# A decay row by DMA in place of four turns, and a reordered front of each DeltaNet head

## The reference

```python
gc = jnp.cumsum(g, axis=-1)                       # log decay within a chunk of 64
diff = gc[..., :, None] - gc[..., None, :]
decay_incl = jnp.exp(jnp.where(incl, diff, -jnp.inf))
m = jnp.einsum('bhnid,bhnjd->bhnij', kb, k) * decay_strict
sol = lax.linalg.triangular_solve(eye + m, rhs, left_side=True, lower=True)
attn = jnp.einsum('bhnid,bhnjd->bhnij', q, k) * decay_incl
qd = q * jnp.exp(gc)[..., None]
...
o = rmsnorm(o, head_norm) * jax.nn.silu(g_out...)
```

## Time and profile before

| | us |
|---|---|
| median of 3 runs | 2720.67 (2720.61 to 2720.92) |
| profiled execution | 2720.52 |
| its span | 2718.7 |
| TensorE busy | 2705.3 |
| VectorE busy | 1581.7 |
| ScalarE busy | 1100.1 |
| GpSimd busy | 258.2 |

### The profile page before, as it was taken

The page is one execution under the profiler, slowest core; times in us unless marked ns, Lnnn a source line. Parts: engine busy times, 40 slices in busy tenths (PEclk is TensorE's granted clock), DMA queues, the critical chain, the costliest instruction groups (busy, mean ns, idle before and its releaser), DMA issues.

```text
span 2718.7 us, 35832 instructions
## 1 busy us (share of the span) xinstructions
PE 2705.3 (100%) x13096; PEld 2251.9 (83%) x13096; DVE 1581.7 (58%) x2504; ACT 1100.1 (40%) x1849; POOL 258.2 (9%) x231
## 2 busy tenths in 40 slices
PE   9999999999999999999999999999999999999998
PEld 7888878888887888888888888788888878888887
DVE  6554357888885345553355543688888943455532
ACT  4222247766663232222222222566676622322222
POOL 0000022122120010000000000211212100100000
PEclk9999999999999999999999999999999999999999
DMA  4223335554542222233322233455556332222332
GB/s 166 96 97 104 92 101 140 130 142 111 136 126 93 98 88 100 93 101 93 102 93 93 100 93 96 108 131 140 125 124 145 96 108 93 93 100 93 97 94 66
DMA packets 84603, 292.04 MB, mean 107 GB/s; under 512 B 10001, under 2 KB 12689, under 8 KB 84497
## 3 DMA queue, kind: packets, MB, share of 16 engines
q1 hardware_dynamic: 69232, 235.85, 26.5%
q0 software_dynamic: 14976, 54.53, 10.9%
q10 hardware_dynamic: 288, 0.27, 0.0%
HBM read 233.99 MB, written 2.10 MB: 87 GB/s over the span
## 4 chain that ended last, share of the span: by engine, by line
PE 97%; DVE 2%; ACT 0%; issue 0%; DMA 0%; DVEq 0%; POOLq 0%; POOL 0%; ACTq 0%
PE bank L438 95%; PE bank L637 1%; PE bank L689 1%; DVE c_lo L1747 0%; DVE w_lo L1235 0%; ACT c_hi L1191 0%; PE bank L651 0%; PE bank L725 0%; DVE sqb L1743 0%; DVE hf L1743 0%; DMA pcol<-in_params_in 0%; DVE hf L1738 0%; PE bank L458 0%; DVE NT L1664 0%; ACT w_hi L855 0%
## 5 line engine op out<-in xcount | busy, mean ns | idle before, releaser
L1235 DVE TENSOR_TENSOR w_lo<-raw,w_hi 128x1024 fp32r<-128x1024 f32 x342 | 422.6, 1237 | 542.2 <-ACT w_hi L855 542.1
L855 ACT ACTIVATE w_hi<-raw 128x1024 fp32r<-128x1024 f32 x446 | 469.8, 1055 | 658.7 <-PE bank L438 658.6
L438 PE MATMUL bank<-h_hi,w_hi 128*128 128x512 f32 x1504 | 587.1, 390 | 2.2 <-DVE h_lo L1260 2.1
L438 PE MATMUL bank<-h_hi,w_lo 128*128 128x512 f32 x1504 | 585.5, 389 | 0.0
L438 PE MATMUL bank<-h_lo,w_hi 128*128 128x512 f32 x1504 | 585.3, 389 | 0.0
L438 PE MATMUL bank<-g_hi,w_hi 128*128 128x512 f32 x928 | 384.2, 414 | 0.0
L438 PE MATMUL bank<-g_hi,w_lo 128*128 128x512 f32 x928 | 378.7, 408 | 0.0
L438 PE MATMUL bank<-g_lo,w_hi 128*128 128x512 f32 x928 | 369.6, 398 | 0.0
L438 PEld LDWEIGHTS bank<-h_hi,w_hi 128*128 128x128 f32 x1504 | 282.3, 188 | 63.3 <-issue 3.6
L438 PEld LDWEIGHTS bank<-h_hi,w_lo 128*128 128x128 f32 x1504 | 282.3, 188 | 58.8
L1535 DVE SCALAR_TENSOR_TENSOR cacc<-c_raw,ncol,cacc 128x512 f32<-128x512 f32 x464 | 330.0, 744 | 0.4
(11 more groups left out here) (258 smaller groups left out, 3355.5 us busy)
## 6 DMA issues: line engine op xcount, KB each, us to landing
raw<-in_w_in SPq DMA_DIRECT2D x128, 512.0 KB, 3.3
w_lo<-raw POOLq DMA_DIRECT2D x104, 512.0 KB, 4.6
raw<-in_ffn_w_gate SPq DMA_DIRECT2D x88, 512.0 KB, 3.2
raw<-in_ffn_w_up SPq DMA_DIRECT2D x88, 512.0 KB, 3.2
raw<-in_ffn_w_down SPq DMA_DIRECT2D x64, 512.0 KB, 3.5
raw<-in_ffn_w_down SPq DMA_DIRECT2D x32, 384.0 KB, 3.1
raw<-in_w_a_out SPq DMA_DIRECT2D x16, 512.0 KB, 3.2
raw<-in_w_b_out SPq DMA_DIRECT2D x16, 512.0 KB, 3.2
```

Source lines behind the costliest of these rows:

```text
L438: return nc.tensor.matmul(o, a, b, start=start, stop=stop, **kw)
L855: nc.scalar.activation(w_hi[c % SLOTS][:, :], raw[c % SLOTS][:, :], ACT.Copy).then_inc(hi_done, 1)
L1235: tt(w_lo[c % SLOTS][:, :], raw[c % SLOTS][:, :], w_hi[c % SLOTS][:, :].bitcast(F32), ALU.subtract).then_inc(lo_v, 1)
```

## The change

In the 14 later heads the four turns `gr` no longer run. At the first head of each layer a copy of gc of all heads is turned once on TensorE into 32 rows (bank 5), copied by ScalarE and written by a DMA to a scratch in HBM (`gc_rows`). For each later head a DMA issued by GpSimd reads its row back, the same row to all 128 partitions, into `dec`, after y3 of the head before. The exponential eg reads this row, and stands ahead of osq at the end of the head before. dmin reads `dec` instead of bank 0.

In the first head of a layer, eg comes ahead of ksq. On TensorE `so` moves behind `x2t`, and vt comes after one more `H`; two more `H` stand in front of x2t. On VectorE og and vE move behind vT. On GpSimd the sum of squares waits for dmin, and qd for vT.

```diff
-PE_ORDER = "H H gr kt H kk kq H so H H H x2t vt H H H xt0 y0 H H fb xy0".split()
+PE_ORDER = "H H gr kt H kk kq H H H H H H x2t so H vt xt0 y0 H H fb xy0".split()
...
-ACT_STEPS = ["thk", "thq", "XTI", "thv", "ksq", "eg", "decT", "kd", "n0", "n1"]
+ACT_STEPS = ["thk", "thq", "XTI", "thv", "eg", "ksq", "decT", "kd", "n0", "n1"]
...
+        gc_rows = nc.dram_tensor("gc_rows", (DEPTH, HEADS * NC, P), F32, kind="Internal").ap()
...
-                        m.then_inc(*pe_dn.step(name))
+                        m.then_inc(gr_done, 1)
+                        nc.tensor.transpose(bank[5][0:HEADS * NC, 0:P], abw[:, 4, :, :].rearrange("p h c -> p (h c)"), ident).then_inc(gct_pe, 1)
...
+                    if name == "gr" and rn != l * 8:
+                        return
...
+                    if rn == l * 8:
+                        act.wait_ge(gr_done, l + 1)
+                        nc.scalar.activation(qd[:, :], bank[0][:, :], ACT.Exp).then_inc(*ac_dn.step("eg"))
                     pe_("kt")
...
-                    nc.scalar.activation(qd[:, :], bank[0][:, :], ACT.Exp).then_inc(*ac_dn.step("eg"))
...
+                    if rn == l * 8:
+                        act.wait_ge(gct_pe, l + 1)
+                        nc.scalar.activation(S[0:HEADS * NC, :], bank[5][0:HEADS * NC, 0:P], ACT.Copy).then_inc(gct_a, 1)
...
                     pe_("os3")
+                    if not gates:
+                        act.wait_ge(row_in, (rn + 1 - l) * 16)
+                        nc.scalar.activation(qd[:, :], dec[:, :], ACT.Exp).then_inc(*ac_dn.step("eg"))
...
+                nc.vector.tensor_copy(abw[:, 4, :, :], sums[:, 0])
...
-                        pe_("gr")
+                        ac("eg")
+                        me("hs")
                         for c in range(NC):
-                            a = stt(out=dec[:, c * P:c * P + P], in0=bank[0][:, c * P:c * P + P], scalar=hs[:, HS_GC, c:c + 1], in1=cst[:, I_CAP, :],
+                            a = stt(out=dec[:, c * P:c * P + P], in0=(bank[0] if rn == l * 8 else dec)[:, c * P:c * P + P], scalar=hs[:, HS_GC, c:c + 1], in1=cst[:, I_CAP, :],
...
-                        if before:
-                            tail("og", rn - 1)
                         ac("ksq")
...
+                        act_of("v", va, va, thv)
                         if before:
+                            tail("og", rn - 1)
                             tail("vE", rn - 1)
-                        act_of("v", va, va, thv)
...
+                                    if rn == l * 8:
+                                        dve.wait_ge(gct_out, (l + 1) * 16)
...
-                            pool.wait_ge(pe_dn.sem, pe_dn.after(rn, "gr"))
+                            ve("dmin")
                             square_sum(rn - 1)
                         ac("eg")
-                        ve("neg")
+                        ve("vT" if before else "neg")
...
+                        if t == 0 and rn is not None and rn != l * 8 + 7:
+                            if rn == l * 8:
+                                pool.wait_ge(gct_a, l + 1)
+                                pool.dma_start(out=gc_rows[l], in_=S[0:HEADS * NC, :]).then_inc(gct_out, 16)
+                                pool.wait_ge(gct_out, (l + 1) * 16)
+                            pool.wait_ge(pe_dn.sem, pe_dn.after(rn, "y3"))
+                            h = rn + 1 - l * 8
+                            row = gc_rows[l, h * NC:h * NC + NC, :].rearrange("(o c) i -> o (c i)", o=1)
+                            pool.dma_start(out=dec[:, :], in_=row.broadcast_to([P, SEQ])).then_inc(row_in, 16)
```

More of the change, by code:

```diff
@@ L96 @@
 assert PE_ORDER.count("H") == 6 * HALVES, PE_ORDER.count("H")
-PE_STEPS = [x for x in PE_ORDER if x not in ("H", "so", "fb")]
+PE_STEPS = [x for x in PE_ORDER if x not in ("H", "gr", "so", "fb")]
 PE_TAIL = ["so", "fb"]
@@ L246, in trunk @@
         ghi_done = sem("ghi_done")
+        gr_done = sem("gr_done")
+        gct_pe = sem("gct_pe")
+        gct_a = sem("gct_a")
+        gct_out = sem("gct_out")
+        row_in = sem("row_in")
         mrinv_done = sem("mrinv_done")
```

## The result

| | before | after |
|---|---|---|
| median, us | 2720.86 (6 runs) | 2731.9 (6 runs) |
| profiled span, us | 2718.7 | 2729.4 |
| TensorE busy, us | 2705.3 | 2706.0 |
| TensorE idle ahead of xy0, as printed | none | 10.5 in 14 heads |

The change made the kernel slower by 11.0 us, a ratio of 1.0041 with a 95% interval of 1.0028 to 1.0053. The predicted 2722.5 and its range of 2717 to 2729 were too low; slower had been given 0.18.

A forecast was written before the change was run, and what follows sets the result against it. TensorE, busy 2705.3 of 2718.7 us, was taken as the bound. Twelve later heads +2.5, last heads 0, first heads -1.3, just in time +0.4, qd's touch 0.2: +1.8, so 2722.5 us, range 2717 to 2729.

The forecast's parts named there:

- There is a catch: VectorE beside GpSimd's sum: bnk2, with two SBUF inputs, ends 0.05 to 0.1 us behind the sum.
- The turns and the order: TensorE, later heads: without gr and with so directly behind x2t, a head would be 0.45 us shorter.
- x2t's wait: TensorE, later heads: x2t has 0.1 us to spare; a just-in-time start adds 0.4 us over 14 heads.
- xy0's wait: TensorE: xy0 waits 0.61 us for VectorE's yd0, 0.66 us a head with the longer matmul behind the wait.
- the wait as 0.21 shorter: Last head of each layer: no dcol, so the wait at xy0 is 0.21 us shorter, 0.45.
- 0.91 us of waiting a head: Upper case of the wait at xy0, with vE's start 0.25 us later: total +4.5 us.
- Rival B: GpSimd's sum, taking 1.8 us, becomes what x2t waits for, x2T 0.5 late: +7.4 us, 2728.1; chance 0.16.
- Rival A: No wait at xy0, VectorE's four taps covered: -7.6 us, 2713.1; chance 0.10, including a wait under 0.14 us.
- C: The power behind vE takes the port ahead of the first tap: taps 1.2 us later, 17 us, 2739; chance 0.04.
- D: The row lands late or never clears y3 in time, delaying the exponential ahead of osq: 2730 and more; chance 0.03.
- The first heads' 1.3 us: TensorE, first heads: two H more in front cover 0.63 us of waiting for x2T and vT, 1.3 us gained.

The follow-up runs named there:

- the run of 2714.06: Changed kernel with so two H behind kq, qd behind neg, og ahead of skE, vE ahead of vT: 2714.06 us, ratio 0.9975 to the kernel before.

## Why the prediction was wrong

The step that failed is the one headed by "There is a catch": that beside a GpSimd product only VectorE instructions with two SBUF inputs are held, so that skE would run at its usual length and bnk2 wait. Its instance, bnk2, was right, as the run with skE on a bank shows, but skE comes first and is held too, to 514.06, and so is dcol, to 518.80. By its terms, per later head:

- The turns and the order: 0.45 us less predicted. In the run of 2714.06 it is 0.42, with so alone among the projections, so the 0.02 for its place isn't in it.
- x2t's wait: 0.03 predicted, 0.31 measured (0.25, and 0.06 in its turns). skE held until the sum's end puts rden, bnk2 and neg behind it, instead of neg alone.
- xy0's wait: 0.66 predicted, 1.00 measured (0.93, and 0.07 in the matmuls behind it). The chain named was right: so, vE, dcol, four taps, yd0, xy0. vE started 0.03 behind so's end and the taps took 2.66. What was missing is dcol at 0.42 instead of 0.18, held by qd, and 0.14 us from yd0 to xy0 where I took 0.06.
- That makes 0.28 + 0.25 + 0.08 = 0.61 us a head, 14 x 0.61 = 8.5 of the 9.4 us between forecast and result. Another 0.2 is the kernel before, 2720.67 in the three runs of the forecast and 2720.86 in all six. I haven't found the rest in one place.

In a layer's last head, where there is no dcol, the first tap was held instead, so those heads gained nothing either (VectorE, then GpSimd):

```profile
768.20 3.23 DVE L1554 SCALAR_TENSOR_TENSOR cacc<-c_raw,ncol,cacc 128x512 f32<-128x512 f32 x4
```

```profile
767.60 1.29 POOL L1897 TENSOR_TENSOR qd<-qd,qT 128x512 f32<-128x512 f32 x1 [3.74 <-DVE va L1655]
```

Here the prediction didn't apply its own rule. Without dcol its first tap, which has two SBUF inputs, would have started at 517.72, while qd ran to 518.0, and yet it took the wait as 0.21 shorter.

One sum is wrong by its own terms: with 0.91 us of waiting a head the total is 1.8 + 14 x 0.25 = +5.3 us, not +4.5. The result lies beyond both.

Rival B, the sum as what x2t waits for, described part of it: it asked for a sum of 1.8 us and x2T 0.5 us late; the sum took 1.27, x2T was about 0.35 late, and the reason was skE beside it. Rival A is refuted by 14 waits. C didn't happen: the power behind qd took 1.04 us, and the taps kept their pace. Nor did D: the row was issued at 532.87, the rows land 4.9 us after their issue in the median, and this one is read at 560.39, more than 20 us later. The first heads' 1.3 us came as said.

The Trainium skill ("SBUF — State Buffer", section "SBUF: two separate sides") names two kinds of VectorE instruction that meet GpSimd at the shared ports: those with two SBUF inputs, and those in a 2-port perf mode. I used the first half and left the second out. Here the runs agree with the first half (bnk2, dmin). They fit the second: the SBUF-to-SBUF TENSOR_SCALAR of float32, held in skE and dcol, is also the kind that takes 0.42 us for 128x512 where products take 0.69 (VectorE, changed kernel):

```profile
526.24 0.42 DVE L1739 TENSOR_SCALAR o_hi<-ssq 128x512 fp32r<-128x512 f32 x1
...
526.97 0.69 DVE L1742 TENSOR_TENSOR o_lo<-ssq,o_hi 128x512 fp32r<-128x512 f32 x1
```

That skE and dcol are held is what the rows show. That they are because of such a mode is inferred from this pace, and no run here shows the mode itself.

The same page says that whoever starts first holds the pair for the whole instruction. For products that GpSimd began first, that is what the rows show; the taps beside GpSimd's powers of four elements keep their pace (and 518.84 in the changed kernel), so for these small instructions no run here shows a hold.

## What to carry to other kernels

When a wait is moved on one engine, lay the lists of the two engines that share a port side by side at the new time, and look at every instruction in the overlap, the tiny ones first: a 0.17 us add became 1.13 us and made x2t late. Moving the input of an instruction from a bank to SBUF changes what may run beside it: dmin, reading `dec`, was held by a sum beside it (2.16 us instead of 1.14). Yet sending the sum behind dmin was dearer by 3.6 us, since it then held skE. Two late arrivals in series hide each other: so's place was worth nothing that can be told alone (0.2 us) and 5.6 once qd was out of the way, so try such edits together before one is dropped.

## What was not expected of the hardware

- Beside a GpSimd product of 128x512 (1.27 us), a VectorE TENSOR_SCALAR of four columns from SBUF to SBUF took 1.13 us (0.17 by itself), a TENSOR_TENSOR with two SBUF inputs 0.76 (0.16 by itself), both to the product's end; a RECIPROCAL from SBUF took 0.18 and a TENSOR_SCALAR from a bank 0.16, as without it.
- In the changed kernel TensorE waited for both x2T and yd0, but x2t started 0.06 us behind x2T's end and xy0 0.14 behind yd0's. No run here tells why.
